# Gate and up by Strassen's seven products, down as a stage of its own

## What is computed

```python
def rmsnorm(x, g):
    return (_normalize(x) * g.astype(jnp.float32)).astype(x.dtype)

def swiglu(h, w_gate, w_up, w_down):
    return (jax.nn.silu(h @ w_gate) * (h @ w_up)) @ w_down
...
        xp = xp + mix_out(y_conv, y_fox, y_mem, out_norm_g[l], w_out[l])
        xp = xp + swiglu(rmsnorm(xp, norm2_g[l]), w_gate[l], w_up[l], w_down[l])
...
    y_prompt = rmsnorm(xp, final_norm_g)
```

## Time and profile before

| | us |
|---|---|
| median of 3 runs | 3116.23 (3107.03 to 3117.82) |
| profiled execution | 3105.9 |
| its span | 3104.2 |
| `combine`, first to last turn of a tile | 1316.87 to 1507.76 |
| `ffn`, first issue to the end of the span | 1529.14 to 3104.2 |
| `ffn`, matmuls | 1561.07 to 3092.31 |
| mean granted TensorE clock | 0.975 |

### The profile page before, as it was taken

How to read it: one execution, slowest core, us unless ns; L and a number is a source line. 1 busy time by engine, 2 the same in 40 slices (tenths; PEclk the granted TensorE clock), 3 DMA queues, 4 the chain that set the end, 5 groups by cost and what they waited for, 6 DMA issues and landing times. The chain is left out here.

```text
span 3104.2 us, 38969 instructions
## 1 busy us (share of the span) xinstructions
PE 2855.5 (92%) x14254; PEld 2409.8 (78%) x14254; DVE 1465.0 (47%) x1762; ACT 1065.7 (34%) x1778; POOL 1014.2 (33%) x561
## 2 busy tenths in 40 slices
PE   6999979778989887499799999999999999999998
PEld 5998878767777676387678888888888888888876
DVE  4366665467777776475323332333324332322222
ACT  3322311456666666321223222332223222222211
POOL 2476667499888882265100000000000000000001
PEclk9999999889999999799899999999999999999999
DMA  4587878566676652564333333443334433233222
GB/s 159 189 261 215 284 216 285 150 178 168 177 187 176 181 148 55 170 218 168 106 105 122 96 102 95 130 142 95 100 118 122 123 102 95 82 109 104 80 82 69
DMA packets 390747, 447.26 MB, mean 144 GB/s; under 512 B 149631, under 2 KB 277690, under 8 KB 389526
## 3 DMA queue, kind: packets, MB, share of 16 engines
q1 hardware_dynamic: 390270, 443.73, 47.7%
q0 software_dynamic: 288, 1.05, 0.1%
HBM read 399.81 MB, written 44.88 MB: 143 GB/s over the span
## 5 line engine op out<-in xcount | busy, mean ns | idle before, releaser
L2097 DVE TENSOR_TENSOR w_items_lo<-w_items,w_items_hi 128x1024 fp32r<-128x1024 f32 x264 | 323.4, 1225 | 1029.5 <-ACT w_items_hi L2008 1029.5
L2008 ACT ACTIVATE w_items_hi<-w_items 128x1024 fp32r<-128x1024 f32 x264 | 279.8, 1060 | 1106.4 <-PE ps_ffn L2260 722.0
L2258 PE MATMUL ps_ffn<-h_hi,w_items_hi 128*128 128x512 f32 x1408 | 550.2, 391 | 1.5 <-DVE h_lo L2119 1.5
L2260 PE MATMUL ps_ffn<-h_hi,w_items_lo 128*128 128x512 f32 x1408 | 549.2, 390 | 0.0
L2259 PE MATMUL ps_ffn<-h_lo,w_items_hi 128*128 128x512 f32 x1408 | 548.7, 390 | 0.0
L863 PE MATMUL ps_proj<-w_hi,h_hi 128*128 128x428 f32 (+1 forms) x800 | 290.7, 363 | 25.8 <-ACT proj_out L611 25.7
L2260 PEld LDWEIGHTS ps_ffn<-h_hi,w_items_lo 128*128 128x128 f32 x1408 | 264.8, 188 | 56.1
L2258 PEld LDWEIGHTS ps_ffn<-h_hi,w_items_hi 128*128 128x128 f32 x1408 | 264.8, 188 | 55.8 <-issue 1.9
L2259 PEld LDWEIGHTS ps_ffn<-h_lo,w_items_hi 128*128 128x128 f32 x1408 | 265.0, 188 | 53.9
L865 PE MATMUL ps_proj<-w_hi,h_lo 128*128 128x428 f32 (+1 forms) x800 | 286.3, 358 | 0.0
L864 PE MATMUL ps_proj<-w_lo,h_hi 128*128 128x428 f32 (+1 forms) x800 | 285.9, 357 | 0.0
(11 more groups left out here) (272 smaller groups left out, 5145.3 us busy)
## 6 DMA issues: line engine op xcount, KB each, us to landing
shared_pages<-in_cache_k SPq DMA_DIRECT2D x256, 256.0 KB, 3.3
page_v<-in_cache_v SPq DMA_DIRECT2D x256, 256.0 KB, 3.0
w_items<-in_w_gate SPq DMA_DIRECT2D x88, 512.0 KB, 3.8
w_items<-in_w_up SPq DMA_DIRECT2D x88, 512.0 KB, 3.8
w_items<-in_w_down SPq DMA_DIRECT2D x88, 512.0 KB, 3.8
shared_pages<-out_proj SPq DMA_DIRECT2D x48, 512.0 KB, 7.0
w_raw<-in_w_in SPq DMA_DIRECT2D x44, 428.0 KB, 4.9
out_proj<-proj_out SPq DMA_DIRECT2D x80, 214.0 KB, 4.0
```

The source lines that it names most:

```text
L2008: act.activation(hi[:, g % RING, :], raw[:, g % RAW, :], ACT.Copy).then_inc(s.w_hi, 1)
L2097: dve.tensor_tensor(lo[:, g % RING, :], raw[:, g % RAW, :], hi[:, g % RING, :].bitcast(F32), ALU.subtract).then_inc(s.w_lo, 1)
L2258: pe.matmul(out, a_hi, h_hi[:, dd, :], start=(dd == 0), stop=False)
L2260: mm = pe.matmul(out, a_lo, h_hi[:, dd, :], start=False, stop=(dd == DT - 1))
```

## The change

`combine` also makes what gate and up read. After the residual, ACT squares the tile of x1 (L1631), Pool makes 1/root (`x_root`, L1579 and L1581), ACT scales the tile by it (L1633), PE turns it (`turn_x`, 8 transposes), DVE multiplies by the gain from PSUM (`turned_x`) and SP stores it to `h2_turned`, (D, TOKENS) in DRAM. x1 holds the 8 sampled rows too (TOKENS = 2056).

`ffn` is replaced by two stages. `gate_up` takes the tokens in three runs (WIDTHS 344, 344, 340, twice each) and, in each run, the weights as 66 items of 256 output columns, gate and up by turns. An item is a product of a 2x2 block matrix of weights with a 2x2 block matrix of tokens, made with seven products of halves in Winograd's form of Strassen's algorithm: four combinations T1 to T4 of weights (Pool), four combinations S1 to S4 of tokens, once a run (DVE in the first run, Pool in the next two), seven products of 12 matmuls each, and seven additions (DVE) after a copy of the first product (ACT). The splits of an item: T1 to T4 by ACT and DVE, b11, b21 and b22 by ACT (`base_hi`) and Pool (`base_lo`). The activations go to `act_turned` in DRAM. The raw weights have two buffers, and so have hi and lo; the combinations have one. `down` holds half of w_down in SBUF at a time (22 tiles of 128x512, split once) and goes over the 16 tiles of tokens for each half; a tile of activations is loaded, split, and multiplied by 66 matmuls of 512 columns, and each half begins with 44 matmuls for the sampled rows.

```diff
+                def x_root(k):
+                    n = rows_of(k)
+                    pool.wait_ge(s.x_squared, k + 1)
+                    pool.tensor_scalar(rstd_x[0:n, k:k + 1], ss_x[0:n, k:k + 1], 1.0 / D, EPS, ALU.mult, ALU.add).then_inc(s.x_var, 1)
+                    pool.wait_ge(s.x_var, k + 1)
+                    pool.tensor_tensor(rstd_x[0:n, k:k + 1], rstd_x[0:n, k:k + 1], c.minus_half[0:n], ALU.pow).then_inc(s.x_rstd, 1)
...
+                    if k >= 2:
+                        x_root(k - 2)
...
+                    act.wait_ge(s.res, k + 1)
+                    if k >= 1:
+                        act.wait_ge(s.h_turned, 2 * k)
+                    act.activation(xn[0:n, :], x[0:n, k % 3, :], ACT.Square, accum_out=ss_x[0:n, k:k + 1]).then_inc(s.x_squared, 1)
+                    act.wait_ge(s.x_rstd, k + 1)
+                    act.activation(xn[0:n, :], x[0:n, k % 3, :], ACT.Copy, scale=rstd_x[0:n, k:k + 1]).then_inc(s.x_normed, 1)
...
+                    normalise_x(k - 1)
+                normalise_x(N - 1)
...
+                def turned_x(k):
...
+                        dve.wait_ge(s.h_turned, 2 * k + j + 1)
+                        dve.tensor_tensor(h_out[:, k % 2, 4 * j:4 * j + 4, 0:n], ps_t[:, j, 0:4 * n].rearrange("p (d t) -> p d t", d=4),
+                                          gain_t[:, 4 * j:4 * j + 4].unsqueeze(2).to_broadcast([P, 4, n]), ALU.mult).then_inc(s.h_made, 1)
...
+                        if d == 1 and k >= 2:
+                            turn_x(k - 2)
...
-def ffn(nc, c, io, scratch):
...
+WIDTHS = (344, 344, 340)
+STARTS = (0, 688, 1376)
+HALVES = ("a11", "a12", "a21", "a22")
+ORDER = ("b11", "t2", "t3", "t1", "b21", "t4", "b22")
+SLOT = {"t2": 0, "t3": 1, "t1": 2, "t4": 3, "b11": 4, "b21": 5, "b22": 6}
+TOKENS = SEQ + DB
...
+def gate_up(nc, c, io, scratch):
...
+                if name == "s1":
+                    eng.wait_ge(s.h_in, 64 * (sc + 1))
+                    eng.tensor_tensor(x[S1], x[S3], x[A22], ALU.add).then_inc(s.s_step, 1)
+                elif name == "s2":
+                    eng.wait_ge(s.s_step, step + 1)
+                    eng.tensor_tensor(x[S2], x[S1], x[A11], ALU.subtract).then_inc(s.s_step, 1)
+                elif name == "s3":
+                    eng.wait_ge(s.s_step, step + 2)
+                    eng.tensor_tensor(x[S3], x[A11], x[S3], ALU.subtract).then_inc(s.s_step, 1)
+                else:
+                    eng.wait_ge(s.s_step, step + 3)
+                    eng.wait_ge(s.h_lo, M * sc + 2)
+                    eng.tensor_tensor(x[S2], x[A12], x[S2], ALU.subtract).then_inc(s.s_step, 1)
...
+                    b = raw[:, g % 2]
+                    b11, b12, b21, b22 = b[:, 0:H, 0:P], b[:, 0:H, P:2 * P], b[:, H:DT, 0:P], b[:, H:DT, P:2 * P]
+                    t = {name: combo[:, SLOT[name]] for name in ("t1", "t2", "t3", "t4")}
+                    pool.wait_ge(w_in[g % 2], 16 * (g // 2 + 1))
+                    if g >= 1:
+                        pool.wait_ge(s.t_lo, g)
+                    pool.tensor_tensor(t["t1"], b12, b11, ALU.subtract).then_inc(s.t_step, 1)
+                    pool.tensor_tensor(t["t3"], b22, b12, ALU.subtract)
+                    pool.wait_ge(s.t_step, 2 * g + 1)
+                    pool.tensor_tensor(t["t2"], b22, t["t1"], ALU.subtract).then_inc(s.t_step, 1)
+                    pool.wait_ge(s.t_step, 2 * g + 2)
+                    pool.tensor_tensor(t["t4"], b21, t["t2"], ALU.subtract).then_inc(s.t_made, 1)
...
+                def base_lo(g):
+                    pool.wait_ge(s.b_hi, g + 1)
+                    b, hi, lo = raw[:, g % 2], w_hi[:, g % 2], w_lo[:, g % 2]
+                    at, last = SLOT["b11"], SLOT["b22"]
+                    pool.tensor_tensor(shape(lo[:, at:at + 2]), b[:, :, 0:P], shape(hi[:, at:at + 2]).bitcast(F32), ALU.subtract)
+                    pool.tensor_tensor(lo[:, last], b[:, H:DT, P:2 * P], hi[:, last].bitcast(F32), ALU.subtract).then_inc(s.b_lo, 1)
+                combos(0)
+                base_lo(0)
+                combos(1)
+                for g in range(N):
+                    base_lo(g + 1)
+                    combos(g + 2)
+                    sc, i = g // ITEMS + 1, g % ITEMS
+                    if sc < SC:
+                        if i in (8, 12, 16):
+                            s_combo(pool, sc, ("s1", "s2", "s3")[(i - 8) // 4])
+                        if i == ITEMS - 1:
+                            s_combo(pool, sc, "s4")
...
+                def combos_hi(g):
...
+                    act.wait_ge(s.t_made, g + 1)
+                    if g >= 2:
+                        act.wait_ge(s.done, M * (g - 1))
+                    act.activation(shape(w_hi[:, g % 2, 0:4]), shape(combo[:]), ACT.Copy).then_inc(s.t_hi, 1)
...
+                def base_hi(g):
...
+                    act.activation(shape(hi[:, at:at + 2]), b[:, :, 0:P], ACT.Copy)
+                    act.activation(hi[:, last], b[:, H:DT, P:2 * P], ACT.Copy).then_inc(s.b_hi, 1)
...
+                    if g + 1 < N:
+                        combos_hi(g + 1)
+                    act.wait_ge(s.done, done(g, "b11"))
+                    if g >= 2:
+                        act.wait_ge(s.c11, g - 1)
+                    act.activation(first[:, b, 0:n], product(g, "b11"), ACT.Copy).then_inc(s.p1, 1)
+                    if g + 1 < N:
+                        base_hi(g + 1)
...
+                def combos_lo(g):
...
+                    dve.wait_ge(s.t_hi, g + 1)
+                    dve.tensor_tensor(shape(w_lo[:, g % 2, 0:4]), shape(combo[:]), shape(w_hi[:, g % 2, 0:4]).bitcast(F32), ALU.subtract).then_inc(s.t_lo, 1)
...
+                def quarter(g, name, base, which, read):
...
+                    dve.tensor_tensor(dst, base, product(g, name), ALU.add).then_inc(read, 1)
+                    if is_up(g):
+                        dve.wait_ge(read, g + 1)
+                        dve.wait_ge(s.silu, 4 * q + {3: 1, 0: 2, 1: 3, 2: 4}[which])
+                        weighed = dve.tensor_tensor(dst, dst, sil[:, which, 0:n], ALU.mult)
+                        if which == 2:
+                            weighed.then_inc(s.act, 1)
...
+                    dve.wait_ge(s.p1, g + 1)
+                    dve.wait_ge(s.done, done(g, "t2"))
+                    dve.tensor_tensor(u2[:, b, 0:n], product(g, "t2"), first[:, b, 0:n], ALU.add).then_inc(s.u2, 1)
+                    if g + 1 < N:
+                        combos_lo(g + 1)
+                    dve.wait_ge(s.done, done(g, "t3"))
+                    dve.wait_ge(s.u2, g + 1)
...
+                    pe.wait_ge(s.t_lo, g + 1)
+                    pe.wait_ge(s.b_lo, g + 1)
+                    for m, name in enumerate(ORDER):
...
+                        acc = product(g, name)
+                        for d in range(H):
+                            a_hi, a_lo = w_hi[:, b, SLOT[name], d, :], w_lo[:, b, SLOT[name], d, :]
+                            pe.matmul(acc, a_hi, h_hi[:, m, d, 0:n], start=d == 0, stop=False)
+                            pe.matmul(acc, a_hi, h_lo[:, m, d, 0:n], start=False, stop=False)
+                            mm = pe.matmul(acc, a_lo, h_hi[:, m, d, 0:n], start=False, stop=d == H - 1)
+                        mm.then_inc(s.done, 1)
...
+def down(nc, c, io, scratch):
...
+                    sp.dma_start(act_raw[:, n % 2], scratch.act_t.rearrange("(f p) t -> p f t", p=P)[:, :, t * P:(t + 1) * P]).then_inc(a_in[n % 2], 16)
...
+                        acc = ps[:, n % 4, :]
+                        pe.matmul(acc, a_hi[:, n % 2, f, :], w_hi[:, f, :], start=first, stop=False)
+                        pe.matmul(acc, a_hi[:, n % 2, f, :], w_lo[:, f, :], start=False, stop=False)
+                        mm = pe.matmul(acc, a_lo[:, n % 2, f, :], w_hi[:, f, :], start=False, stop=end)
...
```

## The result

The changed kernel takes 3125.6 us (median of 7 runs, 3120.8 to 3128.25), the kernel before 3112.5 in 7 runs: a ratio of 1.0039, 95% interval 1.0026 to 1.0051. I had said 3092 and faster. The time lies within my range, but no gain came: the kernel is 0.4% slower, and the sum was 38.5 us short.

The account below looks back on a forecast made before the run. Weight supply through Pool, ACT and DVE was to bound `gate_up`, not PE. Feed-forward terms summed to 1521.2 against 1575.1 (−53.9); `combine` +30 made net −24, span 3080, execution 3082, plus 10.3: 3092, range 3045 to 3150.

Parts of the forecast that it names:

- `down`'s term: `down`, first to last matmul: 2200 matmuls of 512 columns on PE at 0.2268, 499.0 us, 499.5 with the folds.
- The supply of weights: `gate_up`: feeding split weights and combinations takes 964 us against PE's 866.5, losing 98 of the 165 us gained on PE.
- the round through Pool: `gate_up`: one item's chain over Pool, ACT and DVE takes 13.85 or 14.4 us by turns, against PE's 13.2.
- the conflict: `gate_up`: Pool's split of the base blocks waits for DVE's split of the combinations, as both engines take turns at SBUF.
- Rival (a): `gate_up`: PE stays the bound, conflict hidden or Pool's instructions cheaper in a row; median 2995; chance 0.12.
- (b): `gate_up`: Pool's instructions cost 9% more than the best rows, round 15.0, 53 us more, 3145; chance 0.18.
- (c): `combine`: every tile pays ACT's wait for Pool's root and more, +50 us, 3112, no difference to be told; chance 0.10.
- `combine`: The stage `combine` grows by 30 us, between 20 and 45; at 20 only PE's share and the end count.
- ACT's loop: `combine`: ACT's work, with its wait for Pool's root, closes a loop of 13.8 us a tile; 22 us for ten tiles.
- The ends: Feed-forward: 29 us to `gate_up`'s first matmul, 21.6 from its last to `down`'s first, 7.1 for the tail.
- the changes of run 10 each for 11: `gate_up`: each of the two changes between runs of tokens costs 11 us (5 to 20), for splitting seven token blocks.
- The median: Whole kernel: 10.3 us added to the execution of 3082, as the runs' median stood above the profiled execution before; gives 3092.

Follow-up runs that it names:

- the first experiment: Changed kernel, with SP in `down` issuing the load of activations one step earlier, ahead of the store and the residual rows: 3088.6 us, ratio 0.9917.
- The seventh: Changed kernel, with ACT copying an item's base blocks ahead of its combinations, nothing moved between engines, `down` untouched: 3077.8 us, `gate_up` 907.5.
- the tenth experiment: Changed kernel with order alone edited: base blocks first on ACT, loads ahead of stores in `gate_up` and `down`; nothing moved between engines: 3018.8 us, ratio 0.9708.
- the small part on DVE: Changed kernel, with only the smaller lo part of the base blocks (128x512 an item) moved from Pool to DVE: 3091.3 us in one run, `gate_up` 930.3.
- the last experiment: Changed kernel, leaving out in `combine` the square of x1 on ACT and the 1/root on Pool: 3128.2 us in one run.
- the second: Changed kernel, with four buffers in place of three for the rows of x1 in `down`, SP's order untouched: 3106.3 us in one run.

## Why the prediction was wrong, and where it was right

**The step that failed is `down`'s term**, "`down` has 32 × 66 + 88 = 2200 matmuls of 512 columns: × 0.2268 = 499.0". It is a count of PE's work, and I put it in the sum as the stage's time, with no reason why nothing else should bind. For `gate_up` I had followed the order of Pool, ACT and DVE; for `down`, after its cold start, no engine's. The store, the residual rows and the load of activations stand in one queue, each with a wait, and that closed a chain of 18.0 us, 3 more than PE's tile of 14.96. The term came out 40.6 us too small, 540.1 for 499.5, more than the whole miss of 38.5. 36 of them are the chain, as the first experiment shows by opening it (504.1); the other 4.6 lie beside the starts of the two halves and stay. With the chain open the ratio is 0.9917, a time of 3088.6 where I had predicted 3092. That this comes so near is in part luck: its profiled span is 3089.8 where my sum had 3080, and the 10.3 that I added for the median hides it.

Most of the chain's parts were to be had: the copy (I had 2.7), the subtraction (3.1), the normalisation (1.28). The load wasn't: I had 5.5 for it at the cold start, and it took 7.9 there and 8.0 in the chain. With 5.5 the chain would be 15.4 us, less than half a microsecond over PE's tile. So two things failed: I didn't read SP's list, and I took the load at the best rate of the whole kernel.

**The supply of weights was right**, by its steps: the round through Pool, the conflict between the base blocks and DVE's split, and 964 for 962.9. Pool and DVE took turns (3.47 for 2.42) where the order of instructions said. (The two rounds, 13.85 and 14.4, average 14.13; the prediction went on with 14.2, and 14.19 was measured.) But what I made of it was too strong: I wrote that the work "is laid on Pool, the slowest of the engines for it". The seventh and the tenth experiment leave all of that work on Pool, and in the tenth every item away from the changes of run takes PE's own 13.26 or 13.06. The limit was the order on ACT. Rival (a), PE-bound in `gate_up`, was one edit of order away in the first two runs of tokens, two in all three, and not a matter of Pool's price. The rule of the Trainium skill's "GPSIMD Engine Reference", Engine selection, to put elementwise work on VectorE, would have spoken for taking the work off Pool. In the order of the changed kernel that pays: the small part on DVE gave 33 us. With the order put right it doesn't: order alone has `gate_up` at 895, with the small part on DVE it is 900.

**Rivals (b) and (c) were wrong.** The time measured is nearer to their 3145 and 3112 than to my 3092, but not for their reasons. Pool's 512-wide instructions took 1.28 in a row, just the best rows' price, and more only beside DVE's multiplications. The dearer row held waits: of L1215's eight, six took 2.37 to 2.40, and two 3.23 and 3.24, each started while DVE's L1399, with both inputs in SBUF, was running. And `combine` grew by 27, not by (c)'s 50.

**`combine` was right in its size, wrong in its mechanism.** 30 against 26.8, of which 3.1 lay ahead of its first turn (1299.60 against 1296.48), in stages that are the same code. (The table of times before gives 1316.87 as the first turn; that is the second tile's.) I had ACT's loop at 13.8 in ten tiles, for 22 us; ten times 2.0 is 20. It binds in four (13.6 to 14.6 from turn to turn, 12.7 to 13.2 without the square and the root) and costs 5.4 us by the last experiment; the rest is PE's own share, 0.9 a tile, 12.4 in all, and an end that is 5.8 longer. That is close to the case of my lower bound, 20, in which the loop doesn't bind and only PE's share and the end count.

**The ends**: entry 27.7 for 29, exit and ramp 24.0 for 21.6 (the load of activations took 7.9, where I had 5.5), tail 8.2 for 7.1, the changes of run 10 each for 11. **The median**: I added 10.3, the distance of one profiled execution from three runs. In seven runs the kernel before has a median 6.6 above its profiled execution, the changed one 4.8. A profiled execution's distance is noise of one run, so some 4 to 5 us of the forecast were that.

## What to carry to other kernels

Where a stage is replaced, the count of PE's work is a floor, not a term: go down every queue of the new stage, SP's above all, and ask of each load what stands ahead of it and what that waits for. A load that is free to go, behind a store that waits for a result, closes a chain; putting loads ahead of stores was worth 36 us in one stage and 25 in the other. And before work is moved off a slow engine, see whether its steps stand in a row only because of the order on a third engine: one such swap was worth 55 us of the stage here, where moving all of the work gave 17 and part of it 33.

## What the runs showed that I hadn't expected

- A load of activations of 1408 KB takes 8.0 to 8.2 us in most tiles of the first experiment, and 9.4 in the median and up to 10.8 where a store was issued 0.85 ahead of it, in the second. In the third run of tokens a load of 1024 KB of weights landed in 5.4 us ahead of the stores and in 8.2 behind two that are issued 1 us before it.
- 512-wide subtractions on Pool show 1.56 in place of 1.28 beside DVE's multiplications of 344 with both inputs in SBUF, and those show up to 1.64 where the shortest of them takes 0.51: so short ones, too, are paid for on both sides. DVE's additions of 344 with one input from PSUM kept to 0.49 to 0.52 throughout.
- The stages ahead of `combine`, the same code in all kernels, led to its first turn between 1299.6 and 1312.0 in the profiles of the changed kernel and its variants. These stages weren't touched by any of the edits, so up to 12 us of a run's time has no relation to what was changed, and for single runs only times by stage get past it.
